# The cached context's keys and values, made between the steps of the first modulation

## What is computed

```python
sh1, sc1, g1, sh2, sc2, g2 = modulation(cond, p['w_mod'], p['b_mod'])   # silu(cond) @ w_mod + b_mod
h = rmsnorm(x, p['norm1']) * (1 + sc1) + sh1

proj = h @ p['w_in']                   # split: c_q 384, c_kv 256, k_rope 32, gate_b, gate_c, u (512 each)
q = rmsnorm((rmsnorm(c_q, p['q_a_norm']) @ p['w_q_up']).reshape(.., 8, 96), p['q_norm'])
c_kv = rmsnorm(c_kv, p['kv_a_norm'])
k, v = mla_expand_kv(c_kv, k_rope, p['w_kv_up'], p['k_norm'])
k_ctx, v_ctx = mla_expand_kv(ctx_cache[0], ctx_cache[1], p['w_kv_up'], p['k_norm'])   # cached context
k, v = concat([k_ctx, k]), concat([v_ctx, v])
attn = softmax_attention(q, k, v)
conv = gate_b * short_conv(gate_c * u, p['conv_w'])

def mla_expand_kv(c_kv, k_rope, w_kv_up, k_norm):
    kv = (c_kv @ w_kv_up).reshape(b, n, 8, 64 + 64)
    k_nope, v = kv[..., :64], kv[..., 64:]
    k = rmsnorm(concat([k_nope, broadcast(k_rope)]), k_norm)     # 96 per head
    return k, v
```

## Time and profile before

| | us |
|---|---|
| median of 3 runs | 2210.55 (2209.43 to 2210.74) |
| the profiled execution | 2208.95 |
| its span in the trace | 2207.2 |
| TensorE busy | 2039.5 |
| VectorE busy | 862.5 |
| ScalarE busy | 468.5 |
| start of the first latent product | 37.67 |
| first latent product of tile 1 | 83.41 |

### The profile page before, as it was taken

The page is one execution under the profiler, slowest core; times in us unless marked ns, Lnnn a source line. Parts: engine busy times, 40 slices in busy tenths (PEclk is TensorE's granted clock), DMA queues, the critical chain, the costliest instruction groups (busy, mean ns, idle before and its releaser), DMA issues. The chain is left out here.

```text
span 2207.2 us, 27581 instructions
## 1 busy us (share of the span) xinstructions
PE 2039.5 (92%) x11455; PEld 1431.4 (65%) x11455; DVE 862.5 (39%) x1806; ACT 468.5 (21%) x917; POOL 154.2 (7%) x147
## 2 busy tenths in 40 slices
PE   5999999979999999998799999995998399999998
PEld 2776777755666675443587878782443287878785
DVE  2245445355666663337222222223547522222221
ACT  1222222126566563113000000001222100000000
POOL 0000000000000000001111111101000101111110
PEclk9999999989999999999899999997999599999999
DMA  9201111058444323743767878764321976878782
GB/s 354 89 29 43 48 37 41 25 118 280 171 166 168 133 96 121 278 153 135 285 223 263 298 267 292 262 209 147 143 96 58 345 254 230 299 263 302 260 286 61
DMA packets 159086, 404.30 MB, mean 183 GB/s; under 512 B 12561, under 2 KB 30664, under 8 KB 152818
## 3 DMA queue, kind: packets, MB, share of 16 engines
q1 hardware_dynamic: 142370, 344.30, 43.2%
q0 software_dynamic: 16592, 58.24, 9.1%
HBM read 339.46 MB, written 63.05 MB: 182 GB/s over the span
## 5 line engine op out<-in xcount | busy, mean ns | idle before, releaser
L1905 PE MATMUL experts_gu<-experts_h_t,weights_w_gate 128*128 128x160 f32 x2048 | 302.9, 301 | 4.1 <-issue 4.1
L1905 PEld LDWEIGHTS experts_gu<-experts_h_t,weights_w_gate 128*128 128x128 f32 x2048 | 289.1, 192 | 19.1 <-issue 19.1
L1905 PE MATMUL experts_gu<-experts_h_t,weights_w_up 128*128 128x160 f32 x2048 | 299.9, 300 | 0.0
L1905 PEld LDWEIGHTS experts_gu<-experts_h_t,weights_w_up 128*128 128x128 f32 x2048 | 286.1, 191 | 0.0
L1981 DVE TENSOR_TENSOR experts_hid<-experts_act,experts_gu 128x160 f32<-128x160 f32 x128 | 41.1, 321 | 479.2 <-ACT experts_act L1970 472.6
L1929 PE MATMUL experts_dn<-weights_w_down,experts_hid 128*128 128x512 f32 x512 | 225.8, 594 | 0.0
L513 PE MATMUL proj_cv<-proj_h_t,proj_w_in 128*128 128x256 f32 x960 | 213.9, 381 | 2.6 <-DVE proj_h_t L710 2.6
L1970 ACT ACTIVATE experts_act<-experts_gu 128x160 f32<-128x160 f32 x128 | 38.8, 303 | 830.2 <-PE experts_gu L1905 830.2
L513 PEld LDWEIGHTS proj_cv<-proj_h_t,proj_w_in 128*128 128x128 f32 x960 | 182.7, 192 | 29.2 <-issue 4.7
L1929 PEld LDWEIGHTS experts_dn<-weights_w_down,experts_hid 128*128 128x128 f32 x512 | 94.7, 190 | 113.8 <-issue 113.8
L997 PE MATMUL attn_sc<-attn_keys_s,attn_q_s 96*128 96x512 f32 (+1 forms) x384 | 155.5, 541 | 3.8 <-DVE attn_pr_t L1130 2.8
(11 more groups left out here) (401 smaller groups left out, 2117.2 us busy)
## 6 DMA issues: line engine op xcount, KB each, us to landing
weights_w_gate<-w_gate_l SPq DMA_DIRECT2D x32, 2048.0 KB, 9.5
weights_w_up<-w_up_l SPq DMA_DIRECT2D x32, 2048.0 KB, 17.2
weights_w_down<-w_down_l SPq DMA_DIRECT2D x32, 2048.0 KB, 21.9
attn_w_mod<-w_mod_l SPq DMA_DIRECT2D x40, 1024.0 KB, 6.4
proj_w_in<-w_in_l SPq DMA_DIRECT2D x3, 2048.0 KB, 19.9
proj_x<-x POOLq DMA_DIRECT2D x10, 512.0 KB, 4.0
weights_w_down<-x SPq DMA_DIRECT2D x10, 512.0 KB, 4.6
layer_room_a<-w_mod_l SPq DMA_DIRECT2D x4, 1024.0 KB, 10.3
```

The source lines that it names most:

```text
L1905: last = pe.matmul(gu[j % 2][:, m * SLOTS:(m + 1) * SLOTS], w[u][:, k, j * P:(j + 1) * P], h_t[u][:, k, :], start=(k == 0), stop=(k == KD ...
```

## The change

The latent transposes, `kv_up`, the copies, the key chains and the stores of both cached tiles move ahead of tile 0. TensorE makes the first cached tile's latent transposes before modulation step 4 and its `kv_up` after it, the second's after steps 5 and 6; `x_turns(0)` moves from behind step 3 to ahead of step 7. On SP the loads of the cached latents, `w_kv`, the two head gains and the rotary table move ahead of the last four pieces of the modulation's weights; the two stores of cached values stand behind all loads and ahead of tile 0's stores. The keys of both cached tiles are turned, copied out and stored in tile 0. Cached tile 1 uses the key buffer `k_n` instead of `k_c`. The diff, cut to its core:

```diff
-    CACHED_AT = {3: 0, 5: 1}
+    CACHED = (NT, NT + 1)
...
-        tp_uses, lp_uses, kv_uses = {("x", 0): 0}, {}, {}
+        tp_uses, lp_uses, kv_uses = {("lat", NT): 0, ("lat", NT + 1): 1, ("x", 0): 2}, {("kv", NT): 0, ("kv", NT + 1): 1}, {NT: 0, NT + 1: 1}
...
         def keys(n):
-            return k_n if n < NT else k_c
+            return k_c if n == NT else k_n
...
             def _(sp):
...
                 sp.dma_start(conv_rows[:], ...)
+                sp.dma_start(lat_c[:, :, 0:KVL], t["cache_c_kv_l0"]...).then_inc(lat_in, 16)
+                sp.dma_start(lat_c[:, :, KVL:KVL + ROPE], t["cache_k_rope_l0"]...).then_inc(lat_in, 16)
+                sp.dma_start(w_kv[:], t["w_kv_up_l0"]...).then_inc(w_kv_in, 16)
+                sp.dma_start(q_gain[:], t["q_norm_l0"].partition_broadcast(P)).then_inc(head_gains_in, 16)
+                sp.dma_start(k_gain[:], t["k_norm_l0"].partition_broadcast(P)).then_inc(head_gains_in, 16)
+                sp.dma_start(rope_t[:]..., t["rope"]...).then_inc(rope_in, 16)
                 for n in range(4, KD):
                     mod.load(sp, n)
...
                 part_load(0)
...
+                for n in CACHED:
+                    values_store(n)
                 for n in range(NT):
...
                         keys_store(n - 1)
-                    if n - 1 in CACHED_AT:
-                        keys_store(NT + CACHED_AT[n - 1])
+                    else:
+                        keys_store(NT)
+                        keys_store(NT + 1)
...
             def _(pe):
...
                 for n in range(4):
                     mod.step(pe, n)
-                x_turns(0)
                 pe.wait_ge(conv_in, 16)
...
-                for n in range(4, KD):
-                    mod.step(pe, n)
+                latent_turns(NT)
+                mod.step(pe, 4)
+                pe.wait_ge(w_kv_in, 16)
+                kv_up(NT)
+                mod.step(pe, 5)
+                latent_turns(NT + 1)
+                mod.step(pe, 6)
+                kv_up(NT + 1)
+                x_turns(0)
+                mod.step(pe, 7)
                 mod.turn(pe, 0)
...
                     if n:
                         query_turns(n - 1)
                         key_turns(n - 1)
+                    else:
+                        key_turns(NT)
                     latent_turns(n)
...
                         c_part(n)
-                    if n - 1 in CACHED_AT:
-                        key_turns(NT + CACHED_AT[n - 1])
                     if n == 0:
-                        pe.wait_ge(w_up_in, 32)
+                        key_turns(NT + 1)
+                        pe.wait_ge(w_up_in, 16)
...
-                    if n in CACHED_AT:
-                        latent_turns(NT + CACHED_AT[n])
-                        b_part(n, 0, 1)
-                        kv_up(NT + CACHED_AT[n])
-                        b_part(n, 1, JH)
-                    else:
-                        b_part(n, 0, JH)
+                    b_part(n, 0, JH)
...
             def _(act):
...
-                for n in range(3):
-                    x_square(n)
+                x_square(0)
+                latents_kept(NT)
+                keys_values(NT)
+                x_square(1)
+                key_root(NT)
+                latents_kept(NT + 1)
+                keys_values(NT + 1)
+                key_root(NT + 1)
+                x_square(2)
...
             def _(dve):
...
                 dve.tensor_copy(conv_w[:], cv[0][:, 0:3 * CJ]).then_inc(taps_kept, 1)
+                dve.wait_ge(head_gains_in, 32)
+                dve.wait_ge(rope_in, 16)
+                key_sums(NT)
+                keys_normalised(NT)
                 dve.wait_ge(spread, 1)
                 mod.add_bias(dve, 0)
...
                 ch.settle()
+                key_sums(NT + 1)
+                keys_normalised(NT + 1)
                 modulate(1)
                 normalise_x(2)
+                dve.wait_ge(gains_in, 32)
                 for n in range(NT):
                     compress(n)
-                    if n:
-                        keys_kept(n - 1)
+                    keys_kept(n - 1 if n else NT)
...
-                    if n - 1 in CACHED_AT:
-                        keys_kept(NT + CACHED_AT[n - 1])
+                    if n == 0:
+                        keys_kept(NT + 1)
```

More of the change, by code:

```diff
@@ L314, in projections @@
         w_lat_in, w_up_in, w_part_in = s.sem("w_lat_in"), s.sem("w_up_in"), s.sems("w_part_in", 3)
+        w_kv_in, head_gains_in = s.sem("w_kv_in"), s.sem("head_gains_in")
         gains_in, conv_in, rope_in, lat_in = s.sem("gains_in"), s.sem("conv_in"), s.sem("rope_in"), s.sem("lat_in")
@@ L340, in projections @@
                 count(tp_uses, ("x", 1))
+                count(tp_uses, ("k", NT))
             else:
@@ L344, in projections @@
             count(tp_uses, ("lat", n))
-            if n - 1 in CACHED_AT:
-                count(tp_uses, ("k", NT + CACHED_AT[n - 1]))
+            if n == 0:
+                count(tp_uses, ("k", NT + 1))
             count(lp_uses, ("kv", n))
@@ L350, in projections @@
                 count(tp_uses, ("x", n + 2))
-            if n in CACHED_AT:
-                count(tp_uses, ("lat", NT + CACHED_AT[n]))
-                count(lp_uses, ("kv", NT + CACHED_AT[n]))
-                count(kv_uses, NT + CACHED_AT[n])
         count(tp_uses, ("q", LAST))
@@ L380, in _ @@
                 sp.dma_start(conv_rows[:], t["conv_w_l0"].rearrange("a (j p) -> (a j) p", p=P)).then_inc(conv_in, 16)
+                sp.dma_start(lat_c[:, :, 0:KVL], t["cache_c_kv_l0"].rearrange("(c p) r -> p c r", p=P)).then_inc(lat_in, 16)
+                sp.dma_start(lat_c[:, :, KVL:KVL + ROPE], t["cache_k_rope_l0"].rearrange("(c p) r -> p c r", p=P)).then_inc(lat_in, 16)
+                sp.dma_start(w_kv[:], t["w_kv_up_l0"].rearrange("(k p) f -> p k f", p=P)).then_inc(w_kv_in, 16)
+                sp.dma_start(q_gain[:], t["q_norm_l0"].partition_broadcast(P)).then_inc(head_gains_in, 16)
+                sp.dma_start(k_gain[:], t["k_norm_l0"].partition_broadcast(P)).then_inc(head_gains_in, 16)
+                sp.dma_start(rope_t[:].rearrange("p n a r -> p n (a r)"), t["rope"].rearrange("(n p) r -> p n r", p=P)).then_inc(rope_in, 16)
                 for n in range(4, KD):
@@ L386, in _ @@
                 sp.dma_start(lat_gain[:, QL:QL + KVL], t["kv_a_norm_l0"].partition_broadcast(P)).then_inc(gains_in, 16)
-                sp.dma_start(q_gain[:], t["q_norm_l0"].partition_broadcast(P)).then_inc(gains_in, 16)
-                sp.dma_start(k_gain[:], t["k_norm_l0"].partition_broadcast(P)).then_inc(gains_in, 16)
                 def part_load(part):
@@ L396, in _ @@
                 sp.dma_start(w_q[:], t["w_q_up_l0"].rearrange("(k p) f -> p k f", p=P)).then_inc(w_up_in, 16)
-                sp.dma_start(w_kv[:], t["w_kv_up_l0"].rearrange("(k p) f -> p k f", p=P)).then_inc(w_up_in, 16)
                 part_load(0)
-                sp.dma_start(rope_t[:].rearrange("p n a r -> p n (a r)"), t["rope"].rearrange("(n p) r -> p n r", p=P)).then_inc(rope_in, 16)
-                sp.dma_start(lat_c[:, :, 0:KVL], t["cache_c_kv_l0"].rearrange("(c p) r -> p c r", p=P)).then_inc(lat_in, 16)
-                sp.dma_start(lat_c[:, :, KVL:KVL + ROPE], t["cache_k_rope_l0"].rearrange("(c p) r -> p c r", p=P)).then_inc(lat_in, 16)
                 def values_store(n):
@@ L440, in _ @@
                     values_store(n)
-                    if n in CACHED_AT:
-                        values_store(NT + CACHED_AT[n])
                 conv_store(PAIRS - 1, 0)
@@ L478, in latent_turns @@
                     for b, lo, hi in ((0, first, 4), (1, 4, 5)):
-                        pe.wait_ge(tp_free[b], tp_uses["lat", n])
+                        wait(pe, tp_free[b], tp_uses["lat", n])
                         for j in range(lo, hi):
@@ L628, in keys_values @@
                     kv = lp[:].rearrange("p (h c) -> p h c", h=HEADS)
+                    if n == 0:
+                        for b in range(2):
+                            act.wait_ge(tp_full[b], tp_uses["k", NT + 1] + 1)
                     ch.add(act.activation(dst[:, :, NOPE:QK], latents(n)[1].unsqueeze(1).broadcast_to([P, HEADS, ROPE]), ACT.Copy))
@@ L725, in keys_kept @@
                 def keys_kept(n):
-                    wait(dve, k_stored, 16 * (kept_before(n) - PT))
+                    wait(dve, k_stored, 16 * kept_before(n))
                     for b in range(2):
@@ L735, in kept_before @@
                 def kept_before(n):
-                    return sum(1 for name, use in tp_uses.items() if name[0] == "k" and use < tp_uses["k", n])
+                    return sum(1 for name, use in tp_uses.items() if name[0] == "k" and name[1] >= PT and use < tp_uses["k", n])
                 def gate(n):
```

12 lines of the change are left out of this document (removed).

## The result

The changed kernel takes 2234.86 us (2233.61 to 2235.37, 4 runs) against 2210.64 of the kernel before (2209.43 to 2213.81, 4 runs). The ratio is 1.0088, with an interval of 1.0068 to 1.0108: slower by 15 to 24 us. In a later series of runs, where the kernel before has a median of 2216.24 and its runs scatter more, it is 1.0087, 1.0057 to 1.0117. The forecast was 2231, the range 2225 to 2238, the sign slower.

The account below looks back on a forecast made before the run. TensorE, busy 92% of the span, was taken as the bound, its projection head waiting for SP's loads. Terms of -12.5, +2.5 and +31 gave +21 us on 2210.55, 2231.5 taken as 2231, range 2225 to 2238.

Parts of the forecast that it names:

- Parts 1 and 2: Cached work leaving tiles 3 to 6 saves 12.5 us; the two key_turns entering tile 0 cost +2.5 us.
- Part 4: Head: first latent product waits for a values store behind all SP loads, about 68.7 instead of 37.67, +31 us.
- Part 3: Head: two kv_up and four latent transposes between modulation steps cost nothing, as TensorE idles there for transfers.
- Rival A: Head: first latent product does not wait for the store; head 4.1 to 8 us longer, 2206.5 as middle; chance 0.11.
- Rival B: Head: rope's slow issue holds up SP, all loads end later, first product near 77, +29 net, 2240; chance 0.04.
- Rival C: Tiles 3 to 6: the gain doesn't come because something else paces them; 2244; chance 0.02.

Follow-up runs that it names:

- the loads alone: Kernel before with only the cached latents, w_kv, head gains and rotary table loaded ahead of the last four modulation weight loads: 2223.26 us, ratio 1.0028.
- the run with the large loads: Kernel before with only the cached latents, their rotary part and w_kv loaded ahead of the last four modulation weight loads: 2218.54 us, ratio 1.0022.
- the lean kernel in its second order: Changed kernel with second value buffer, gains and rotary table loaded later, cached key scaling in tile 0, modulation steps before second kv_up: 2207.62 us, ratio 0.9961.

## Why the prediction was right

The sum held term by term; in the trace it was 20.9 against 21 forecast. The median moved by 24.2, as by the traces the Fourier stretch of layer 1, which the forecast had no term for, added 3.4.

- **Parts 1 and 2.** -12.5 was forecast for tiles 3 to 6; their sum went from 178.94 to 166.38, -12.56. +2.5 for tile 0; it went from 45.74 to 48.22, +2.48. Taking tile 1 as the pattern for the order keys, latents, c part was right: 91.71 to 93.85 is 2.14, against 2.15 there. That tile 0 as a whole hit to a few hundredths is luck: it takes 45.74 and 46.99 in the two traces of the kernel before, 48.22 and 48.93 in those of the changed one.
- **Part 4.** Forecast: landing at about 68, first latent product at 68.7, bounds 64.4 to 73.7. Measured: 67.76 and 68.50. That the wait is the cause is shown by the run without it (54.45), that it is the place in the queue by the run with the store sooner (59.29). The last load landed at 48.33 + 18.8 = 67.1, against 67.0 forecast, and the store 0.6 behind it, at the pace of its bytes. The loads' end came out this close partly by luck: I cancelled 480 KB more against one tile of `x` less, and the sum had no term for the hole of 24 to 27; by the slices it cost the loads' end nothing, because the hole of 36 to 42, of about the same size, had gone, which I had not seen coming.
- **What I had right with a wrong cover.** Part 3 costed the cached products between the steps at nothing and put the price without cover at 2 x 3.60 plus about 1, so 8.2. With the store's wait gone, the first latent product comes at 54.45 with these products and at 46.35 with the loads alone: 8.1. They were not free; the wait of part 4 lay over them. That 8.1 is so near 8.2 is luck: the two `kv_up` took 4.70 and 5.37, with 1.83 of waiting for ScalarE and the transposes beside them, while steps 5 to 7 took 1.04 each where they take 1.89 with the loads alone, and no longer waited 0.6 each for their weights. I had named both covers, waiting for weights and part 4, and only the second held in full.
- **Rival A was priced wrong,** 4.1 to 8 us of head, 2206.5 as its middle. Without the wait the head is 16.8 us longer: 8.7 for the loads, of which 4.9 are small pieces, and 8.1 for the order on TensorE. Even without its fault the change as written would not have been measurably faster (1.0012, 0.9992 to 1.0032). I had the small pieces as an end of a range where they are the larger half of the term.
- **Rival B** came in part: gains and rope did hold SP (3.14, 2.91 and 2.44 us to issue with the loads alone, 5.67 for the load behind them), and the hole came, but the loads ended no later, at 67.1. What the hole cost the modulation's steps lay under the store's wait. **Rival C** fell: tiles 3 to 6 are all at 41.6.

So the 31 us of the head, in the order in which they were uncovered: 8.7 for the loads moved ahead, 8.1 for the cached products ahead of the last steps, and 14.0 for a store that stands behind all loads. These are differences of single traces: the same kernel's start differs by 0.3 to 0.6 us from one trace to the next, and nearly 2 us move from the third part to the second or back with the clock at the second `kv_up`.

## What to carry to other kernels

When work moves earlier, go through the waits that it brings along, not only the ones that it leaves: a wait on a single buffer's store was met long before in tile 3 and became the longest of the stage in the head, as the store's place on SP's queue, behind 6 MB and more of loads, decides when it lands. An engine that idles for transfers is not free room: what is put there in order stands ahead of the next thing that it waits for, and every byte ahead of the awaited one counts, small pieces several times their bytes. The room was where TensorE waits for VectorE, after the last step, and work there also kept its clock up.

## What the runs showed of the hardware

- **Small pieces early in the queue cost more than their bytes.** 48 KB of gains took SP 3.14 us to issue at 8.88 in the run with the loads alone, where the 1024 KB of w_kv took 0.61 just before that. It is not the pieces alone: in the kernel before the same two loads took 0.93 and 0.77, at 27.86 and 28.83. With them ahead, 288 KB cost 4.9 us of the head. The Trainium skill (DMA: Bandwidth & Descriptors, Specifications) says that pieces under 512 bytes don't reach line rate; the runs agree in direction, 239 GB/s with the gains (384 bytes a piece) and the table (128) ahead and 412 without.
- **The granted clock reads 1.00 where the work shows the lower level.** In every trace the first four modulation steps take 1.89 us each, with a clock of 1.00 beside them (12 to 21 in the slices); later the same step takes 1.04, and 1.89 where 0.50 is read (30 to 36 in the run with the large loads). With the loads alone steps 4 to 7 take 1.89 too, and the first latent product 10.98 instead of 9.20, with 1.00 beside them. In the head, then, the durations and not the reading tell which of 1.2 and 2.4 GHz it was.
- **The clock can fall while TensorE is busy.** In layer 1's Fourier stage of the changed kernel a product over 2 partitions and the one behind it took 5.11 and 5.64 us, with a granted clock of 0.66 in 1581 to 1591 and no idle time; in the first trace of the kernel before the same two took 3.69 and 3.70 at 1.00. TensorE went through the same products without idle time in both. The changed kernel's timeline first, then the kernel before:

```profile
1579.15 5.11 PE L2320 MATMUL mix_banks<-weights_w_up,weights_w_gate 2*128 2x512 f32 x8
1584.19 5.64 PE L2306 MATMUL mix_banks<-weights_w_down,weights_w_gate 128*128 128x512 f32 x8
```

```profile
1558.68 3.69 PE L2313 MATMUL mix_banks<-weights_w_up,weights_w_gate 2*128 2x512 f32 x8
1562.31 3.70 PE L2299 MATMUL mix_banks<-weights_w_down,weights_w_gate 128*128 128x512 f32 x8
```

  This place alone is 3.4 us of the difference between the two traces that the projections don't explain. In the ten traces it is slow in the eight of altered kernels, in part or in full, and in neither of the kernel before. It does not come from being late: the lean kernel in its second order, 8 us ahead of the kernel before, has it too (4.48 and 6.27). What decides it is open.
